# Second layer: all attention score products as fp32r halves, the rotary ones as row halves of two heads in turn; last layer: products with a matrix of ones in halves

## The reference, cut to what matters

```
def mla_layer(x, pos, norm_g, w_in, q_norm_g, w_q_up, kv_norm_g, w_kv_up, q_gain, k_gain, w_out):
    ...
    k = jnp.concatenate(
        [k_nope, jnp.broadcast_to(k_pe[:, :, None, :], (b, s, A_HEADS, A_ROPE))], axis=-1)
    q = rms_norm_2(q, q_gain)
    k = rms_norm_2(k, k_gain)
    q = jnp.concatenate([q[..., :A_NOPE], rope(q[..., A_NOPE:], pos)], axis=-1)
    k = jnp.concatenate([k[..., :A_NOPE], rope(k[..., A_NOPE:], pos)], axis=-1)
    o = mla_attend(q, k, v, pos).reshape(b, s, A_WIDTH)
    ...
def diff_layer(...):
    ...
    k = rms_norm_2(k.reshape(b, s, B_HEADS, 2, B_HD), k_gain)
    ...
    o = rms_norm_2(o, subln_g) * (1.0 - lam_init)
```

## Time and profile before

| what | value |
|---|---|
| median of 3 runs | 3378.85 us (3375.01 to 3381.91) |
| the profiled execution | 3381.08 us, its span 3379.3 us |
| PE / PEld / DVE / ACT / POOL busy | 97% / 78% / 52% / 35% / 4% of the span |
| mean granted clock of TensorE | 0.991 of 2.4 GHz |

### The profile page before, as it was taken

One profiled execution on the slowest core, in us unless ns is written; L12 is line 12 of the kernel. 1 busy time (PEld: TensorE's weight loads), 2 busy tenths in 40 slices (PEclk: granted clock), 3 DMA queues, 4 the chain that ended last, 5 costly groups with the idle time before them and its releaser, 6 DMA issues. The chain is left out here.

```text
span 3379.3 us, 52198 instructions
## 1 busy us (share of the span) xinstructions
PE 3289.9 (97%) x22037; PEld 2652.3 (78%) x22037; DVE 1757.7 (52%) x2953; ACT 1197.4 (35%) x1883; POOL 119.6 (4%) x96
## 2 busy tenths in 40 slices
PE   7999999999999989999999999999999999999999
PEld 6877777777777778767786776788888888888887
DVE  5235555545555546364436666433655566655732
ACT  4123343333333322232224444323334344433421
POOL 1000000000001001100000000010000000000000
PEclk9999999999999999999999999999999999999999
DMA  7423333231122135243342112353322233322452
GB/s 238 112 75 91 89 92 91 90 96 56 53 67 77 55 112 154 74 131 83 96 111 78 50 36 85 109 150 112 88 87 88 81 91 90 94 81 88 156 146 84
DMA packets 492525, 324.27 MB, mean 96 GB/s; under 512 B 27130, under 2 KB 448605, under 8 KB 491782
## 3 DMA queue, kind: packets, MB, share of 16 engines
q1 hardware_dynamic: 492294, 320.94, 32.4%
HBM read 276.05 MB, written 44.85 MB: 95 GB/s over the span
## 5 line engine op out<-in xcount | busy, mean ns | idle before, releaser
L530 PE MATMUL PS<-XH,WHT 128*128 128x512 f32 (+1 forms) x2224 | 907.2, 408 | 7.1 <-DVE AR L1027 2.1
L518 DVE TENSOR_TENSOR WLT<-AR,WHT 128x1024 fp32r<-128x1024 f32 (+1 forms) x430 | 520.0, 1214 | 706.9 <-ACT WHT L512 706.1
L532 PE MATMUL PS<-XH,WLT 128*128 128x512 f32 (+1 forms) x2224 | 874.6, 393 | 0.0
L512 ACT ACTIVATE WHT<-AR 128x1024 fp32r<-128x1024 f32 (+1 forms) x430 | 447.1, 1042 | 679.7 <-PE PS L532 498.0
L531 PE MATMUL PS<-XL,WHT 128*128 128x512 f32 (+1 forms) x1712 | 671.5, 392 | 0.0
L530 PEld LDWEIGHTS PS<-XH,WHT 128*128 128x128 f32 (+1 forms) x2224 | 418.9, 188 | 111.2 <-issue 14.8
L532 PEld LDWEIGHTS PS<-XH,WLT 128*128 128x128 f32 (+1 forms) x2224 | 418.5, 188 | 98.1
L531 PE MATMUL PS<-ARR,WHT 128*128 128x512 f32 x1024 | 404.9, 395 | 0.0
L531 PEld LDWEIGHTS PS<-XL,WHT 128*128 128x128 f32 (+1 forms) x1712 | 322.8, 189 | 72.1 <-issue 4.8
L531 PEld LDWEIGHTS PS<-ARR,WHT 128*128 128x128 f32 x1024 | 192.5, 188 | 43.9 <-issue 3.6
L530 PE MATMUL PS<-XL,WHT 128*128 128x512 f32 x512 | 203.0, 397 | 0.1
(11 more groups left out here) (467 smaller groups left out, 5261.9 us busy)
## 6 DMA issues: line engine op xcount, KB each, us to landing
AR<-b_w_in SPq DMA_DIRECT2D x128, 512.0 KB, 4.0
AR<-w_in SPq DMA_DIRECT2D x122, 512.0 KB, 4.0
AR<-a_w_in SPq DMA_DIRECT2D x48, 512.0 KB, 4.3
AR<-w_out SPq DMA_DIRECT2D x32, 512.0 KB, 4.4
AR<-a_w_out SPq DMA_DIRECT2D x32, 512.0 KB, 4.0
AR<-b_w_out SPq DMA_DIRECT2D x32, 512.0 KB, 4.1
proj_scratch<-AR SPq DMA_DIRECT2D x33, 256.0 KB, 2.1
AR<-a_w_kv_up SPq DMA_DIRECT2D x32, 256.0 KB, 3.8
```

The lines of the kernel that those rows point to most:

```text
L512: self.nc.scalar.activation(self.shaped(self.high, n), self.shaped(self.raw, n), ACT.Copy).then_inc(self.s_high, 1)
L518: self.nc.vector.tensor_tensor(self.shaped(self.low, n), self.shaped(self.raw, n), f32(self.shaped(self.high, n)), ALU.subtract).then_inc( ...
L530: mm(out, wh, xh[k0 + c], start=(start and c == 0), stop=False)
L532: last = mm(out, wl, xh[k0 + c], start=False, stop=(stop and c == nk - 1))
```

## The change

All score products of the second layer take fp32r halves. `scores` has for each head three products of 128 partitions, and then three rounds of rotary products, head 0 and head 1 in turn. The halves come from new operations: `key_high` and `rotary_key_high` on ScalarE, `kl0`, `kl1` and `krl` on GpSimd for the keys; for the plain query two instructions on VectorE instead of one (`query_copy`); `rotary_high` on ScalarE and `qrl` on GpSimd for the rotary query. Keys and queries have one buffer now instead of two, so the new copies wait for `scores(i, 3)` ("pe.s3"). On TensorE `query(q, 0)` and `swap(q)` stand ahead of `values(i, 0)`, and `rotary_sums(q)` behind `turned(i, 3)`. On ScalarE `rotary_square(q)` stands ahead of `exps(i, 3)`. On VectorE `scale(i, 3)` stands ahead of `output(i, 0)`. In the last layer the squares for `key_factors` and `out_sums` are split into halves (the ones are exact in fp32r), with the low half on GpSimd, and each product with ones is two fp32r products instead of one float32 product.

```diff
-                    N.wait(pe, i, "dve.cq1", "dve.qa", "dve.kr1")
+                    N.wait(pe, i, "dve.cq1", "pool.krl")
+                    W.wait(pe, i, "pool.qrl")
                     S.wait(pe, i - 1, "dve.b31")
                 else:
                     S.wait(pe, i, f"dve.b{u - 1}1")
                 for e in heads:
-                    mm(SB[e][:, :], QN[i % 2][:, e, blk(u)], KN[i % 2][:, e, :], start=True, stop=False)
-                for e in heads:
-                    last = mm(SB[e][:, :], QRG[rows(e), i % 2, blk(u)], KR[rows(e), i % 2, :], start=False, stop=True)
+                    mm(SB[e][:, :], QNH[e][:, blk(u)], KNH[e], start=True, stop=False)
+                    mm(SB[e][:, :], QNH[e][:, blk(u)], KNL[e], start=False, stop=False)
+                    mm(SB[e][:, :], QNL[e][:, blk(u)], KNH[e], start=False, stop=False)
+                for q, x in ((QRH, KRH), (QRH, KRL), (QRL, KRH)):
+                    for e in heads:
+                        last = mm(SB[e][:, :], q[rows(e), blk(u)], x[rows(e), :], start=False, stop=(q is QRL))
                 S.did(last, "pe", f"s{u}")
...
                     rotary(q)
+                    query(q, 0)
+                    swap(q)
                 else:
                     out_unit(1, 1)
                 values(i, 0)
-                if more:
-                    query(q, 0)
                 turned(i, 2)
                 if more:
-                    swap(q)
                     query(q, 1)
-                    rotary_sums(q)
                 else:
                     out_unit(2, 1)
                 turned(i, 3)
                 if more:
+                    rotary_sums(q)
                     query_sums(q, 0)
...
                 N.wait(act, i, f"dve.cq{e}", f"pe.rk{e}")
-                N.did(A(SQ[:, e, :], QN[i % 2][:, e, :], ACT.Square), "act", f"sq{e}")
+                N.did(A(SQ[:, e, :], FB[1][:, :], ACT.Square), "act", f"sq{e}")
+
+            def key_high(i, e):
+                N.wait(act, i, f"dve.kg{e}")
+                S.wait(act, i - 1, "pe.s3")
+                N.did(A(KNH[e], KF[:, e, :], ACT.Copy), "act", f"kh{e}")
+
+            def rotary_key_high(i):
+                N.wait(act, i, "dve.kr1")
+                S.wait(act, i - 1, "pe.s3")
+                N.did(A(KRH, KRF, ACT.Copy), "act", "krh")
+
+            def rotary_high(i):
+                W.wait(act, i, "dve.qa")
+                S.wait(act, i - 1, "pe.s3")
+                W.did(A(QRH, QRF, ACT.Copy), "act", "qrh")
...
                 if not more:
                     high(i - 1)
+                if more:
+                    key_high(q, 0)
+                    key_high(q, 1)
+                    rotary_key_high(q)
+                    rotary_square(q)
                 exps(i, 3)
-                if more:
-                    rotary_square(q)
-                copy(i, 2)
                 if more:
                     query_square(q, 0)
                 st.split_high(act, UT + 4 * i + 6)
                 if more:
+                    rotary_high(q)
+                copy(i, 2)
+                copy(i, 3)
+                if more:
                     query_square(q, 1)
...
+            Pt = nc.gpsimd.tensor_tensor
+            for i in range(NP):
+                for e in heads:
+                    N.wait(pool, i, f"act.kh{e}")
+                    S.wait(pool, i - 1, "pe.s3")
+                    N.did(Pt(KNL[e], KF[:, e, :], f32(KNH[e]), ALU.subtract), "pool", f"kl{e}")
+                N.wait(pool, i, "act.krh")
+                N.did(Pt(KRL, KRF, f32(KRH), ALU.subtract), "pool", "krl")
+                W.wait(pool, i, "act.qrh")
+                W.did(Pt(QRL, QRF, f32(QRH), ALU.subtract), "pool", "qrl")
...
             def key_copy(i, e):
                 N.wait(dve, i, f"pe.k{e}")
-                S.wait(dve, i - 2, "pe.s3")
-                do(f"ck{e}", V.tensor_copy(KN[i % 2][:, e, :], FB[e][:, :]))
+                N.wait(dve, i - 1, f"pool.kl{e}")
+                do(f"ck{e}", V.tensor_copy(KF[:, e, :], FB[e][:, :]))
 
             def query_copy(i, e):
                 N.wait(dve, i, f"pe.qn{e}")
-                S.wait(dve, i - 2, "pe.s3")
-                do(f"cq{e}", V.tensor_copy(QN[i % 2][:, e, :], FB[1][:, :]))
+                S.wait(dve, i - 1, "pe.s3")
+                do(f"cqh{e}", V.tensor_copy(QNH[e], FB[1][:, :]))
+                N.wait(dve, i, f"dve.cqh{e}")
+                do(f"cq{e}", TTn(QNL[e], FB[1][:, :], f32(QNH[e]), ALU.subtract))
...
             def rotary_gain(i):
                 N.wait(dve, i, "pe.qr")
-                S.wait(dve, i - 2, "pe.s3")
-                do("qg", TS(QRG[:, i % 2, :], FB[0][:, :], k.prm("q_gain", 1), None, ALU.mult))
+                W.wait(dve, i - 1, "pool.qrl")
+                do("qg", TS(QRF, FB[0][:, :], k.prm("q_gain", 1), None, ALU.mult))
...
                 bias(i, 3)
                 if more:
                     rotary_gain(q)
-                output(i, 0)
                 if more:
                     query_copy(q, 0)
                     rotary_turn(q)
+                    scale(i, 3)
+                output(i, 0)
                 st.split_low(dve, UT + 4 * i + 6)
-                scale(i, 3)
                 if more:
...
                 if b < BH - 2:
-                    pe.wait_ge(g_os, b + 1)
-                    mm(MB[:, :], C("ones"), TM[:, 0, :], start=True, stop=True).then_inc(p_osq, 1)
+                    pe.wait_ge(g_olo, b + 1)
+                    mm(MB[:, :], k.ONESR[:, :], TMH, start=True, stop=False)
+                    mm(MB[:, :], k.ONESR[:, :], TML, start=False, stop=True).then_inc(p_osq, 1)
...
+                if p == 0:
+                    pe.wait_ge(v_ones, 1)
                 for c in HALF:
-                    pe.wait_ge(a_sq, 4 * p + 2 + c + 1)
-                    mm(OB[c][:, :], C("ones"), SQ[:, c, :], start=True, stop=True).then_inc(p_rk, 1)
+                    pe.wait_ge(g_sqlo, 2 * p + c + 1)
+                    mm(OB[c][:, :], k.ONESR[:, :], SQH[:, c, :], start=True, stop=False)
+                    mm(OB[c][:, :], k.ONESR[:, :], SQL[:, c, :], start=False, stop=True).then_inc(p_rk, 1)
...
+            def out_squares(b):
                 pool.wait_ge(a_os, 2 * b + 2)
-                nc.gpsimd.tensor_tensor(TM[:, 0, :], TM[:, 0, :], TM[:, 1, :], ALU.add).then_inc(g_os, 1)
+                Pt(TM[:, 0, :], TM[:, 0, :], TM[:, 1, :], ALU.add).then_inc(g_os, 1)
+                pool.wait_ge(g_os, b + 1)
+                nc.gpsimd.tensor_copy(TMH, TM[:, 0, :]).then_inc(g_ohi, 1)
+                pool.wait_ge(g_ohi, b + 1)
+                Pt(TML, TM[:, 0, :], f32(TMH), ALU.subtract).then_inc(g_olo, 1)
+            for p in range(BH):
+                if p >= 2:
+                    out_squares(p - 2)
+                for c in HALF:
+                    pool.wait_ge(a_sqhi, 2 * p + c + 1)
+                    Pt(SQL[:, c, :], SQ[:, c, :], f32(SQH[:, c, :]), ALU.subtract).then_inc(g_sqlo, 1)
...
+            def square_high(p, c):
+                act.wait_ge(a_sq, 4 * p + 2 + c + 1)
+                if p:
+                    act.wait_ge(v_gate, 2 * p)
+                Ac(SQH[:, c, :], SQ[:, c, :], ACT.Copy).then_inc(a_sqhi, 1)
```

More of the change, by code:

```diff
@@ L2334, in tiles @@
         return take(n * T, w).rearrange("p (a t) -> p a t", t=T)
-    KN, QN = ([tiles(2) for _ in halves] for _ in range(2))
-    QRG, KR, SQ, SWS = tiles(2), tiles(2), tiles(3), take(T)
+    KNH, KNL, QNH = ([k.EXTR[:, 2 * n + j, :] for j in halves] for n in range(3))
+    QRH = k.EXTR[:, 6, :]
+    QNL = [k.ARR[:, j, :] for j in halves]
+    QRL, KRH, KRL = (k.ARR[:, n, :] for n in (2, 3, 4))
+    take(5 * T)
+    KF, KRF, QRF, SGT = tiles(2), take(T), take(T), tiles(2)
+    take(T)
+    SQ, SWS = tiles(3), take(T)
     XA, XB = (x[:, 0:8, :] for x in (k.XHF, k.XLF))
@@ L2366, in latent @@
     N = Marks(k, "mlap",
[L2367 to L2369 removed]
+              pe=["k0", "k1", "kn", "rk0", "rk1", "qr", "qn0", "qn1", "qrs", "qns"],
+              act=["sk0", "sk1", "rootk", "kh0", "kh1", "krh", "sqr", "sq0", "sq1", "rootq"],
+              pool=["kl0", "kl1", "krl"],
+              dve=["ck0", "ck1", "meank", "reck", "dg0", "dg1", "kg0", "kr0", "kg1", "kr1", "qg", "cqh0", "cq0", "cqh1", "cq1", "meanr", "meanq", "recq", "rq"])
+    W = Marks(k, "mlar", pe=["sw"], dve=["sws", "qc", "qa"], act=["qrh"], pool=["qrl"])
     V_ = Marks(k, "mlav", pe=["a", "b"], act=["a", "b"])
@@ L2498, in key @@
                 if i:
-                    N.wait(pe, i - 1, ("dve.sws", "dve.cq1")[e])
+                    if e:
+                        N.wait(pe, i - 1, "dve.cq1", "act.sq1")
+                    else:
+                        W.wait(pe, i - 1, "dve.sws")
                 else:
@@ L2532, in query @@
                 if e:
-                    N.wait(pe, i, "dve.cq0")
+                    N.wait(pe, i, "dve.cq0", "act.sq0")
                 else:
@@ L2539, in swap @@
                 N.wait(pe, i, "dve.qg", "act.sqr")
```

(11 more changed lines are left out.)

37 lines of the change are left out of this document (20 added, 17 removed).

## The result

The changed kernel takes **3361.39 us**, the median of four runs (3355.3 to 3365.98), against 3379.32 us of the kernel before, measured beside it: a ratio of 0.9946, with an interval from 0.9935 to 0.9958. 3363 was forecast. The execution that was profiled takes 3358.49 us, its span 3356.7, which is 22.6 less than the span of before.

The account below looks back on a forecast made before the run. PE was taken to bound the kernel, busy 49.26 of 50.33 us an iteration and 700.00 of 700.00 in the last layer. Second layer -7.4 and last layer -8.8 made -16.2 us: 3364.9 profiled, median 3363 us, range 3355 to 3373.

Parts of the forecast that it names:

- score step: Second layer, 32 steps: each falls from 2.87 to 2.34 us, a gain of 0.53, with head row halves side by side.
- kl0 asks: Second layer: POOL's low key half asks at 1952.35, during DVE's first multiplication of `scale(i, 2)`, and runs from 1952.66 to 1953.82.
- the swap starts: PE, second layer: `swap(q)` starts at 1958.47 after PE waits 1.36 us, in seven iterations.
- The order of the wait: Second layer: kl0 holds DVE's second multiplication, DVE is 0.86 us late, then "qg", "sqr" and swap follow; PE waits 1.36.
- Second layer: Seven iterations at -0.76 us, first `scores(0, 0)` -0.5, three steps of the last iteration -1.6: together -7.4 us.
- Last layer: Products with ones in halves: -0.80 us eight times and `out_sums` -0.40 six times, -6.4 and -2.4; PE never idle.
- The sum: Second and last layer together: -16.2 us, from 3381.08 to 3364.9 us profiled, median 3363 us.
- POOL missing the gap: Rival, second layer: kl0 asks after 1952.76, DVE isn't late, swap waits 0.50 us; 3357 us, chance 0.14.
- No overlap: Rival, score steps: fp32r row halves don't run side by side, each step 0.17 us longer; 3375 us, chance 0.11.
- POOL first: Rival, second layer: kl0 asks before 1952.17, both multiplications held, DVE 1.9 us late; 3370 us, chance 0.15.
- Entering and leaving at each change of head: Rival, score steps: each 64-row fp32r product pays 0.20 us by itself, a step 1.18 longer; 3408 us, chance 0.05.
- The rule of the ports: SBUF port pair shared by DVE and POOL: exclusive lock for an instruction; counted as 0.86 us more wait an iteration.

Follow-up runs that it names:

- POOL late: Changed kernel, but kl0 on GpSimd waits until the second multiplication of `scale(i, 2)` is done: 3358.26 us, ratio 0.9941.
- when forced: Changed kernel with the rotary products of both heads reading rows 0 to 63: 3374.47 us, ratio 0.9987.
- an edit at another place, factors early: Changed kernel with `key_diagonals` ahead of `bias(i, 2)` on DVE and value copies ahead of `exps(i, 2)` on ACT: 3378.70 us, ratio 1.0001.
- the edit at `key_factors`: `key_diagonals` ahead of `bias(i, 2)`, value copies ahead of `exps(i, 2)`: 3378.70 us on the changed kernel, 3341.89 us with `swap(q)` also behind `values(i, 0)`.
- the swap late: Changed kernel with `swap(q)` behind `values(i, 0)` on PE, and DVE and ACT orders to match: 3353.33 us, ratio 0.9924.
- old order: Changed kernel with `query(q, 0)` again behind `values(i, 0)` and `swap(q)` behind `turned(i, 2)`, DVE and ACT to match: 3378.45 us, ratio 0.9991.
- old order, sums too: Halves kept, `query(q, 0)` and `swap(q)` in their former places, `rotary_sums(q)` also back between `query(q, 1)` and `turned(i, 3)`: 3364.88 us, ratio 0.9961.

## Why the prediction was right

Times are counted from the start of `scores(i, 3)`, 1949.13 in the earlier trace rows and 1942.17 - 2.38 = 1939.79 after. (The row of its first product starts at 1939.39 but is drawn out to 0.79 us; the next starts at 1940.02, one spacing of 0.23 behind 1939.79.)

| step | forecast | measured |
|---|---|---|
| score step | 2.34 | 2.38 |
| first multiplication of `scale(i, 2)` starts | 3.04 | 3.04 |
| kl0 asks | 3.22 | 3.26 |
| second multiplication ends | 4.98 | 4.96 |
| PE has finished `query(q, 0)` | 7.98 | 7.99 |
| "qg" ends | 8.52 | 8.51 |
| the square starts and ends | 8.61, 9.19 | 8.54, 9.14 |
| the swap starts | 9.34 | 9.28 |
| from there to `scores(q, 0)` | 10.55 | 10.60 |

- **The order of the wait** was right in every link: the second multiplication is held and the first isn't, and the swap is late by 1.29 us from start to start, for 1.36. The 0.07 are ACT, which begins the square 0.03 behind "qg", not 0.09. "qa", `exps(i, 3)`, `scale(i, 3)` and `qrl` reach no wait, as said, though the second multiplication of `scale(i, 3)` is held too (1.60 us), by qrl.
- **The score step** was rounded the wrong way. 1.38, 0.09 and 0.89 made 2.36, I took 2.34, and it is 2.38. The gain of a step is 0.49 and not 0.53, over 32 steps 1.3 us too much.
- **Second layer.** 32 x 0.49 - 7 x 1.29 = 6.7 us, for 7.4. From the start of the first score step to the end of the last (381.2 us before, 372.6 after), the trace has 8.6, of which 1.7 is a stretch at the lower clock of before at 2119.7 us that is absent after: 6.9 remain.
- **Last layer.** The ones products take 4 x 0.23 = 0.93 us a head, and in place of the earlier trace rows stands

```profile
2910.35 0.39 PE L3451 MATMUL PS<-STGR,ONESR 128*128 128x512 f32 x1
2910.58 0.40 PE L3452 MATMUL PS<-SQR,ONESR 128*128 128x512 f32 x1
2910.82 0.39 PE L3451 MATMUL PS<-STGR,ONESR 128*128 128x512 f32 x1
2911.05 0.39 PE L3452 MATMUL PS<-SQR,ONESR 128*128 128x512 f32 x1
2911.28 0.40 PE L534 MATMUL PS<-XH,WHT 128*128 128x512 f32 x1
```

  A head gives 1.28 instead of 1.20, and PE is never idle. The products themselves gave what was forecast: from the first of them to the second product behind them it takes 1.17 us after for 1.95 before at `key_factors`, and 0.69 for 1.09 at `out_sums`, 1.18 together; and from the first head to the second, where no `out_sums` lies between, the distance falls from 99.65 to 98.87 us, 0.78. The 0.1 more gathers over the unchanged fp32r products in between, most of it in the first 20 us behind `key_factors`; why they stand a little closer together stays open. With it the last layer gave about 9.3 us (8.5 from the first `key_factors` to the last, and 0.8 for the last one), for 8.8.
- **The sum.** The profiled executions differ by 22.6, of which 6.6 is the clock; 16.0 remain, for 16.2. Half a microsecond too much in the second layer and half too little in the last cancelled. The median fell by 17.9. That it was met to 2 us owes something to luck, for the medians carry the clock's stretches.
- **The rivals.** POOL missing the gap is what the run with POOL late makes: 0.45 us late at the swap for 0.50, and 3358.26 us for 3357. No overlap would have cost a rotary part of 1.58 us, and does when forced. POOL first was not far off: the gap that kl0 must hit is 0.2 us wide on that side, and an edit at another place pushed it over. Entering and leaving at each change of head never showed.
- **The rule of the ports**, one exclusive lock for DVE and POOL (the Trainium skill, SBUF — State Buffer, "SBUF: two separate sides"), spoke against the change, and the trace agrees: a hold of 0.84 us in each of seven iterations. What it cost was a matter of what stood behind it.

## What to carry to other kernels

Ask of each operation added to an idle GpSimd which VectorE operation with SBUF operands runs at that moment, and what waits behind that one: the same 0.84 us cost all of it where TensorE was waiting already, and nothing where the 3.45 us of `values` lay between. A reordering and a cheaper product that come in one change should be timed apart; here the halves earned 2.0 us an iteration and the place of the swap gave 1.3 of it back. And a wait moved away is safe only once the next link has slack: the edit at `key_factors` was worth -1.5 us with the swap late and +2.5 with it early.

## What the runs showed that I had not expected

- **Who holds whom can't be read from the starts of rows alone.** The second multiplication of `scale(i, 3)` has its row from 1952.92 in the changed kernel, 0.05 us before that of qrl on POOL (1952.97, 1.27 us), and yet it is the one held: it takes 1.60 us and ends at 1954.52, 0.28 behind qrl, and so in all seven iterations. A lead of 0.22 us was enough to escape: the first multiplication of `scale(i, 2)` starts at 1942.83, kl0's row at 1943.05.
- **The lower clock follows waits at one place and not at another.** Idle times of 0.45 and 0.53 us close together ahead of the sums were followed by 3.41 us at 1.2 GHz in five of the six iterations that have both (old order), and 0.45 and 0.38 in one of six (old order, sums too). With single ones of 3.01 it began within the wait or right behind it, seven times of seven (factors early); single ones of 1.13 and 1.32 were followed by none. In the old order a slow stretch cost 1.5 us, more than both waits. What decides stays open.
- **Row halves don't need neighbours.** Three products on rows 0 to 63 and then three on rows 64 to 127 start in three pairs, 0.33 and 0.23 us apart, just as with heads in turn. How far ahead this reaches was not tried.
- **Shown idle times are short** by about 0.16 us behind an fp32r product and 0.24 behind a float32 one, since records overlap by that much in unbroken work. The periods agree with the distances of starts: 48.33 + 1.29 = 49.62 for 49.63, and 46.86 + 1.32 + 0.16 = 48.34 for 48.33.
